# A two-layer hybrid block with routed experts: token rows scattered by slot into DRAM instead of gathered by a one-hot product

## The reference

```python
def moe_swiglu(h, w_router, wg, wu, wd):
    logits = (h @ w_router).astype(jnp.float32)
    top_v, top_i = lax.top_k(logits, TOP_K)          # TOP_K = 2 of 8
    top_p = jax.nn.softmax(top_v, axis=-1)
    gates = jnp.sum(jax.nn.one_hot(top_i, N_EXPERTS, dtype=jnp.float32) * top_p[..., None], axis=-2)
    act = jax.nn.silu(jnp.einsum('bnd,edf->bnef', h, wg)) * jnp.einsum('bnd,edf->bnef', h, wu)
    act = act * gates.astype(h.dtype)[..., None]
    return jnp.einsum('bnef,efd->bnd', act, wd)
# h = x * (1 + scale) + shift;  x <- LayerNorm(alpha * x + gate * moe_swiglu(h))
```

## Time and profile before

| what | value |
|---|---|
| runs | 1744.07, 1744.25, 1749.58 us |
| profiled execution | 1745.37 us, span of its instructions 1743.5 us |
| TensorE busy | 1551.2 us, 89% |
| VectorE, ScalarE busy | 761.9 us (44%), 575.6 us (33%) |
| DMA | 425.14 MB, mean 244 GB/s |
| granted TensorE clock, mean | 0.946 |
| expert loop | from 878 to 1708 us |
| chain that ended last | TensorE 75%, DMA 7%, VectorE 6%, SyncE's DMA issues 6% |

### The profile page before, as it was taken

One profiled execution on the slowest core, in us unless ns is written; L12 is line 12 of the kernel. 1 busy time (PEld: TensorE's weight loads), 2 busy tenths in 40 slices (PEclk: granted clock), 3 DMA queues, 4 the chain that ended last, 5 costly groups with the idle time before them and its releaser, 6 DMA issues.

```text
span 1743.5 us, 24616 instructions
## 1 busy us (share of the span) xinstructions
PE 1551.2 (89%) x9147; PEld 1033.1 (59%) x9148; DVE 761.9 (44%) x1228; ACT 575.6 (33%) x979; POOL 75.9 (4%) x92
## 2 busy tenths in 40 slices
PE   4798989999999898989886699989999899999771
PEld 1584567888887585566622366645555577677220
DVE  0483776433333664675700255524544443244115
ACT  0432554332221442451200344433433433233101
POOL 2010001000000010020000000000000000000002
PEclk8799999999999899999789799999999999999896
DMA  9235535442442444565499999999999578677993
GB/s 334 98 133 179 194 121 189 147 139 83 140 145 91 176 145 161 193 194 177 172 379 387 333 389 395 387 382 386 380 337 366 215 286 290 210 270 261 387 389 114
DMA packets 216738, 425.14 MB, mean 244 GB/s; under 512 B 15656, under 2 KB 65832, under 8 KB 216592
## 3 DMA queue, kind: packets, MB, share of 16 engines
q1 hardware_dynamic: 197792, 395.35, 62.7%
q0 software_dynamic: 5264, 18.04, 3.2%
q10 hardware_dynamic: 13536, 9.83, 1.8%
HBM read 406.93 MB, written 16.25 MB: 243 GB/s over the span
## 4 chain that ended last, share of the span: by engine, by line
PE 75%; DMA 7%; DVE 6%; SPq 6%; issue 3%; ACT 3%; ACTq 1%; POOL 0%; DVEq 0%; POOLq 0%
PE ps L2004 27%; PE ps L2406 6%; PE ps L2323 5%; PE ps L2324 4%; PE ps L2327 4%; SPq L717 4%; PE ps L2400 3%; PE ps L2452 3%; DMA hT<-h_columns 2%; PE ps L1936 2%; PE ps L2348 2%; DMA ring<-in_w_moe_up 2%; PE ps L2351 2%; PE ps L2354 2%; PE ps L2098 2%
## 5 line engine op out<-in xcount | busy, mean ns | idle before, releaser
L2004 PE MATMUL ps<-d_ring_parts,scratch_parts 128*128 128x512 f32 (+1 forms) x444 | 172.2, 388 | 13.9 <-DVE hT_parts L1296 9.1
L2400 PE MATMUL ps<-ring,hT 128*64 128x512 f32 (+1 forms) x576 | 128.3, 590 | 38.0 <-issue 21.0
L1840 DVE TENSOR_TENSOR cst<-cst,ps 128x256 f32<-128x256 f32 (+2 forms) x89 | 32.8, 369 | 254.5 <-ACT cst L1151 254.5
L2004 PE MATMUL ps<-gu_ring_parts,scratch_parts 128*128 128x512 f32 (+1 forms) x336 | 128.7, 383 | 0.0
L2406 PE MATMUL ps<-ring,hT 128*32 128x256 f32 x1760 | 117.2, 385 | 7.5 <-DMA hT<-h_columns 7.5
L2004 PE MATMUL ps<-d_ring_parts,hT_parts 128*128 128x512 f32 (+1 forms) x312 | 119.2, 382 | 0.0
L2400 PEld LDWEIGHTS ps<-ring,hT 128*64 128x64 f32 x576 | 40.8, 144 | 112.3 <-issue 84.7
L2004 PEld LDWEIGHTS ps<-d_ring_parts,scratch_parts 128*128 128x128 f32 x444 | 84.8, 191 | 32.2 <-issue 9.3
L2004 PE MATMUL ps<-gu_ring_parts,o_parts 128*128 128x512 f32 x264 | 103.2, 391 | 0.0
L1176 ACT ACTIVATE qkv_parts<-ring 128x1024 fp32r<-128x1024 f32 x102 | 103.1, 1050 | 0.0
L2406 PEld LDWEIGHTS ps<-ring,hT 128*32 128x32 f32 x1760 | 56.3, 110 | 56.5 <-issue 23.8
(11 more groups left out here) (383 smaller groups left out, 3119.8 us busy)
## 6 DMA issues: line engine op xcount, KB each, us to landing
ring<-in_w_moe_gate SPq DMA_DIRECT2D x176, 512.0 KB, 9.9
ring<-in_w_moe_up SPq DMA_DIRECT2D x176, 512.0 KB, 11.4
ring<-in_w_moe_down SPq DMA_DIRECT2D x176, 512.0 KB, 9.8
gu_ring<-in_w_ada SPq DMA_DIRECT2D x48, 1024.0 KB, 7.5
gu_ring<-in_w_in SPq DMA_DIRECT2D x16, 1024.0 KB, 7.3
gu_ring<-in_w_ffn_gate SPq DMA_DIRECT2D x11, 1024.0 KB, 5.4
gu_ring<-in_w_ffn_up SPq DMA_DIRECT2D x11, 1024.0 KB, 7.9
d_ring<-in_w_ffn_down SPq DMA_DIRECT2D x11, 1024.0 KB, 9.8
```

What stands on the lines that cost most here:

```text
L2004: ins = pe.matmul(out, a, w, start=(start and n == 0), stop=(stop and n == 2))
L2400: ins = pe.matmul(ps[64 * j:64 * j + 64, bank, 0:2 * f].rearrange("p (a f) -> p a f", a=2), hT[:, kc, col:col + 64], wt[:, :, f * j:f * j ...
```

## The change

The one-hot table, its product with the rows, the splitting of the rows and the store of the columns go. In their place:

- GpSimd clears a second table in DRAM, `h_table` (1152 rows of 4 KB), with nine DMAs ahead of the ten clears of `y_rows`. After the mixer's norm it stores x in `x_kept`, and when the slots are known, it scatters each tile's rows of h to the two slots of each token: six indirect DMAs.
- x's buffer in SBUF now holds, during the loop, the rows of h of the next body. ScalarE loads them from `h_table` with four DMAs: for the first body after the scatters, and for each other body in step 2 of the body before it.
- TensorE turns rows into columns by transposes into PSUM, from where ScalarE and VectorE copy halves to `hT`: the base (8 transposes) before the last down product of the body before, the other 256 rows (16 transposes) at the common top, before the first gate-up product, and only where the body has a full group. The top now waits for the result's copies first, since those transposes write PSUM banks 0 to 3.
- In the last body x comes back from `x_kept`, and `fold` waits for it.
- SyncE loads granules 10 to 15 right after granule 0.

```diff
             sp.wait_ge(ada_expanded, 32)
             load_granule((0, 0), 0)
-            for first, last, n in ((0, HALF_SLOTS, 4), (HALF_SLOTS, SLOTS_PADDED, 8)):
...
-                sp.dma_start(h_columns[:, :, first:last], hT_all[:, :, first:last]).then_inc(columns_stored, 16)
-            sp.wait_ge(gather_mm, 16)
-            load_granule((0, 0), AHEAD - 1)
-            sp.wait_ge(columns_stored, 32)
...
-            for pos in range(10, AHEAD - 1):
+            sp.wait_ge(stored, 128)
+            for pos in range(10, AHEAD):
                 load_granule((0, 0), pos)
...
                 if l == 1:
+                    for r0 in range(0, SLOTS_PADDED, P):
+                        pool.dma_start(h_table[r0:r0 + P, :].rearrange("r (c f) -> r c f", f=P),
+                                       cst[:, C_ONES:C_ONES + P].unsqueeze(1).broadcast_to([P, KD, P])
+                                       ).then_inc(table_cleared, 16)
                     for r0 in range(0, ROWS_MAX, P):
...
+            pool.dma_start(x_kept, x[:, :, :].rearrange("p i d -> p (i d)")).then_inc(x_stored, 16)
+            pool.wait_ge(table_cleared, 16 * (SLOTS_PADDED // P))
+            pool.wait_ge(slots_ready, 1)
+            for i, n in ((2, 4), (0, 6), (1, 6)):
+                pool.wait_ge(hTok_copied, n)
+                for a in range(2):
+                    pool.indirect_dma_start(h_table[:, :], bass.IndirectOffsetOnAxis(ap=slot_at[:, i, a:a + 1], axis=0),
+                                            h_rows[:, i, :], None).then_inc(rows_scattered, 16)
+            pool.wait_ge(rest_turned, NE)
+            pool.wait_ge(x_stored, 16)
+            pool.dma_start(x[:, :, :].rearrange("p i d -> p (i d)"), x_kept).then_inc(x_back, 16)
...
+            def load_rows(at):
+                for where_at, tall, p0, i in zip(at, (P, P, 64, 64), (0, 0, 0, 64), (0, 1, 2, 2)):
+                    act.dma_start(x[p0:p0 + tall, i, :], h_table[where_at, :]).then_inc(rows_landed, 16)
+
+            def base_columns(n):
+                act.wait_ge(base_turned, n)
+                act.activation(hT[:, 0:4, 0:P], ps[:, 6, :].rearrange("p (k t) -> p k t", k=4), ACT.Copy).then_inc(base_act, 1)
+
+            act.wait_ge(rows_scattered, 16 * 2 * NT)
+            act.wait_ge(x_stored, 16)
+            act.wait_ge(xT_mm, 16)
+            load_rows([slice(0, P), slice(P, 2 * P), slice(2 * P, WIDEST), slice(WIDEST, TOKENS)])
+            base_columns(1)
...
+                        if k == 2 and partner:
+                            act.wait_ge(rest_turned, t + 1)
+                            act.wait_ge(rest_turned, t + 1).then_inc(rows_landed, 16 * LOADS)
+                            next_rows(t + turns)
...
+            def turn_rows(i, banks):
                 for kc in range(KD):
...
+                    ins = pe.transpose(ps[:, banks[kc // 4], P * (kc % 4):P * (kc % 4) + P], x[:, i, P * kc:P * kc + P], ident)
+                return ins
...
+                        if k == len(steps):
+                            pe.wait_ge(hidT_copied, s0 + turns * STEPS)
...
+                                turn_next(t + turns)
...
                 with pe.If(variant > 1):
-                    pe.wait_ge(hT_base, t * 16 + 16)
+                    pe.wait_ge(y_act, t * HELD + HELD)
+                    pe.wait_ge(y_dve, t * HELD + HELD)
+                    turn_rows(1, (0, 1))
+                    turn_rows(2, (2, 3)).then_inc(rest_turned, 1)
+                    pe.wait_ge(base_act, t + 1)
+                    pe.wait_ge(base_dve, t + 1)
```

More of the change, by code:

```diff
@@ L82 @@
 D_GRANULES = 10
-GATHER_BANKS = [0, 1, 2, 3]
+LOADS = 4
 ROW_BANKS = [4, 5, 6, 7]
@@ L1110, in _ @@
                     act.activation(expo[:, :, :], expo[:, :, :], ACT.Exp).then_inc(expo_ready, 1)
-            COLUMNS = [(T_BASE, 0, P, hT_base), (T_REST, P, WIDEST - P, hT_rest), (T_PART, WIDEST, TOKENS - WIDEST, hT_part)]
-            def fetch_columns(t, which):
-                for at, c0, w, landed in which:
-                    first = act.value_load(sched[0:1, bass.ds(t + at, 1)], min_val=0, max_val=SLOTS_PADDED - w)
-                    act.dma_start(hT[:, :, c0:c0 + w], h_columns[:, :, bass.ds(first, w)]).then_inc(landed, 16)
@@ L1849, in expert @@
                     turned_rest(len(steps) - 1)
+                if partner:
+                    dve.wait_ge(base_turned, t + 2).then_inc(base_dve, 1)
+                    base_columns(t + turns + 1)
+                else:
+                    with dve.If(t < NE - 1):
+                        base_columns(t + turns + 1)
+                if partner:
+                    dve.wait_ge(rest_turned, t + 2).then_inc(rest_dve, 1)
+                if ng == 0:
+                    dve.wait_ge(rest_turned, t + 1).then_inc(rest_dve, 1)
                 y0 = t * HELD + HELD * (turns - 1)
@@ L1869, in first_product @@
                 with dve.If(variant > 1):
+                    dve.wait_ge(rest_turned, t + 1)
+                    for q in range(2):
+                        ins = dve.tensor_copy(hT[:, 4:8, P + P * q:2 * P + P * q],
+                                              ps[:, 2 * q + 1, :].rearrange("p (k t) -> p k t", k=4))
+                    ins.then_inc(rest_dve, 1)
                     dve.wait_ge(sil_ready, t * STEPS + (DENSE + 1))
```

207 lines of the change are left out of this document (79 added, 128 removed).

## The result

The changed kernel takes 1750.15 us (median of 11 runs, 1746.41 to 1756.62), the kernel before beside it 1742.23 us (median of 11). The ratio is 1.0036, 95% interval 1.0020 to 1.0052: slower, as forecast, but by half of what I had: 6 us instead of 12.

The account below looks back on a forecast made before the run. TensorE and DMA were taken as both full in pair bodies B and C, with TensorE standing between bodies. The terms summed to +12.0 us on 1744.3, forecasting 1756 us, range 1737 to 1775.

Parts of the forecast that it names:

- term 4: Start of the first pair body (B): rows already in SBUF, so the fetch waits go; -15.6 us.
- term 5: Starts of the second and third pair bodies (C, D): transposes wait for result copies; +3.1 and +1.1 us.
- term 8: First pair body (B): weight ring enters about five granules shorter after a shorter pause; +1 us, bounds 0 and 8.
- term 1: Before the mixer's last norm: nine more clears delay the norm's bias on GpSimd's queue; +18.9 us, bounds 0 and 24.
- Norm to A: Last norm to first body (A): scatters, row loads, transposes and loop entry take 51.4 us, before 57.4.
- term 3: First body (A): 6.1 us of ring waits go, transposes add 1.9 and a branch 1; -3.2 us.
- term 6: Ends of the three pair bodies (B, C, D): transposes of the next base, 1.9 us each; +5.7 us.
- term 7: Third step of pair bodies (B, C, D): ScalarE's table reads and DMA issues partly delay weight splitting; +3 us, bounds 0 and 12.
- term 9: Last body (E): x's return from DRAM, less a dropped column fetch, +3 us; branches around unneeded transposes, +1.
- the norm isn't pushed: Mixer's last norm: parameters land with the old delay, -18.9 us, 1737; chance 0.12. By half: 11.5 us, 1749; chance 0.10.
- the 15 us of third-step issues: Pair bodies (B, C, D): ScalarE's DMA issues held up, 6 us each into the split's chain; +15, 1771; chance 0.12.
- The routing is quicker: Norm to first body: half the loop's entry overlaps and scatters land at once; up to -9 us, 1747; chance 0.08.

Follow-up runs that it names:

- e2: Kernel before, with nine clears of an unused DRAM table put ahead of its ten; ratio to the kernel before 1.0146.
- e1: Changed kernel with its 19 clears spread over the three steps of the attention before; ratio to the kernel before 0.9993.
- e8: Kernel before, with its ten clears of the result's table spread over the three steps of the attention; ratio to the kernel before 1.0002.
- e3: Changed kernel with the ten clears of y_rows moved behind the six scatters; ratio to the kernel before 1.0017.
- e4: Changed kernel with 64 more transposes, results unread, at the end of the first body; ratio to the kernel before 1.0065.
- e5: Changed kernel with the next body's rows fetched ten steps before a pair body's last step, not at its third; ratio to the kernel before 1.0039.
- e9: Changed kernel with clears spread, next rows fetched ten steps before a pair's end, last 6 of 16 granules held until rows land; ratio to before 0.9922.
- e10: Changed kernel with 160 more transposes, results unread, at the end of the first body; ratio to the kernel before 1.0114.
- e7: Changed kernel with clears spread, next rows fetched ten steps before a pair's end, last 4 of 16 granules held until rows land; ratio to before 0.9972.
- e11: Changed kernel with clears spread and the last 6 of 16 granules held until rows land, rows fetched at third step; ratio to the kernel before 0.9949.

## Why the prediction was wrong

The direction and the largest term were right. **The step that failed is the cost of the bodies' starts, terms 4 and 5.** I had -15.6 + 4.2 = -11.4 us, and the marks show -24.1 - 0.4 = -24.5. I took TensorE's work there from rows in which the granted clock was low: 0.50 for the transposes of the earlier trace rows, and 0.73, 0.72 and 0.81 for the base products of B, C and D (9.6, 9.8 and 8.8 us). In the changed kernel's profile the transposes stand ahead of the base product, and this runs at 1.00 and takes 7.0 us each time, 7.1 us less over the three. At B the copies and branches ahead of them took 1.5 us and not 5.5. What B's start won beyond the forecast the stream of weights took back (term 8, of which I saw 1 us in 7.5); what C and D won stayed. The sizes, with what the marks and runs show:

1. **The clears, +18.9: right.** +20.0 in the changed kernel, +20.2 in e2. By the Trainium skill, page "DMA: Bandwidth & Descriptors", section "Anatomy of one DMA — SWDGE (gpsimd) path", an estimate by bytes over 436 GB/s gave +10; e2's norm, 20.2 us later, disagrees with it.
2. **Norm to A, 51.4 us: 48.4 measured.** Between roots and A's first matmul the stretch shrank by 9.1 us. Scatters landed in 6.4 us and loads in 7.3, near the sum; the loop's entry took 4.9 us instead of 9.8. What I had not seen is that this price hangs on term 1: it is low because the clears had let the ring fill first. e1 shows the other price, 10.6 us more. A part of the 9.1 us may be the profiled execution's own, since e2 and e8 have 3 us more than the kernel before here.
3. **A, -3.2: -2.3, near by luck.** The 6.1 us of ring waits did not vanish, 4.9 stayed. Against that, the transposes and the wait ahead of them cost 1.3 us and not 2.9, and the rest of A's products took 2.4 us less, at a mean granted clock of 0.97 instead of 0.94. I let the weights flow at 380 GB/s from A's start. But the ring was full then, and loads can only follow what A frees: 211 GB/s in its first 20 us (389 before, in 882 to 902 us).
4. **Start of B, -15.6: -24.1.** From A's last matmul to the first turn 12.1 us instead of 36.3. I had 9.6 us for the base product, as in the earlier trace rows, where TensorE had stood 17 us and the product's mean granted clock was 0.73; now TensorE stands 1.5 us, the clock stays at 1.00 (2.4 GHz) and the product takes 7.0. The 16 transposes took 1.8 us, not 3.7, at 1.00 too. Copies and branches took 1.5 us, not 5.5; of these, no row shows the 2.5 us that I had added for ScalarE's code. The product's clock is 1.00 at B in e1, e3, e4, e5, e9 and e10 as well.
5. **Starts of C and D, +3.1 and +1.1: +0.4 and -0.8.** The transposes and the wait for copies are there (3.5 and 4.0 us at C), as in the sum, at a granted clock of 0.51 (1.2 GHz, after 4.0 us of standing), but the clock is back at 1.00 for the base product, 7.0 instead of 9.8 us and 8.8, and the fetches' waits go. This part is not steady: in e1, e3, e5 and e10 the first 7 us of C's base product have a clock of 0.81 to 0.93.
6. **Transposes of the next base, +5.7: right in sum,** not in its parts: 1.1 us of transposes (I had 1.9) and 0.8 us of waiting for ScalarE, three times.
7. **Third-step issues, +3: 7.5, and not by that cause.** The added waits for the split are 2.5 us in B and 5.0 in D. e5 takes the issues away: B keeps its length and D keeps 3.2 of its 5.0, all of it the first of the two waits. In every version with turned rows the first wait in D is 3.0 to 3.6 us. VectorE's timeline in D, after, shows it idle for 6.1 us with nothing to wait for before the split's first work (1.6 us in the kernel before):

```profile
1356.81 0.42 DVE L1856 TENSOR_TENSOR cst<-cst,ps 128x256 f32<-128x256 f32 x1 [7.30 <-ACT cst L1258]
1363.38 2.29 DVE L1791 TENSOR_TENSOR hT_parts<-hT,o_parts 128x2048 fp32r<-128x2048 f32 x1 [6.14 <-issue]
```

Why VectorE comes so late is open.

8. **The ring at B, +1: 7.5.** For the head start that I forecast, +1 holds: e4 starts B 7.5 us later, which leaves 16.6 of the 24.1 us, and its B is 164.7 us long, 0.6 more than in e10 (164.0), where 5.7 us are left. The changed kernel's is 171.5 us long for 158.6 before: 7.5 are the head start lost to the ring (against e10), 1.9 are term 6, 2.5 are term 7, 1.0 has no name. I had written that in B and C both TensorE and the DMA are full, and then priced a shorter ring by the length of the pause alone, with no end to what a shorter pause can win. The end is in a pause of the stream that my two windows, which meet at 985 us, don't show. In the kernel before SyncE issued nothing for 12.3 us at B's start, 9.8 of them waiting for TensorE to free a granule: B's late start had let the ring fill. From 985 to 993 us the DMA moved 219 GB/s.

```profile
980.70 0.41 SPq L717 DMA_DIRECT2D ring<-in_w_moe_up  x1
993.00 2.22 SPq L723 DMA_DIRECT2D ring<-in_w_moe_down  x4
```

So the 88th to the 100th of the 528 loads took 30.3 us. In the changed kernel they take 19.4, with no such pause; e4 has none either, and in e10 it is back, 12.5 us. From the 40th load to the 352nd, issued 3.4 us before C's last matmul, the changed kernel's weights flow at 368 GB/s (360 before). The stream won the 11 us of the pause, and from A's last matmul to B's last TensorE won as much, 11.3 us. By the 352nd load the stream is 4.9 us ahead of before, and not 15.

9. **E, +4: -0.6.** E's entry after D took 14.5 us instead of 11.2, but the rest was 3.9 us shorter: TensorE waited 5.4 us for weights there instead of 9.6, so the bytes that I had charged don't show. The same code entered E in 9.0 us in e4 and 13.6 in e5, so this part of the ledger is only known to some 5 us; what sets it is open. E's first matmul after:

```profile
1638.07 12.24 PE L2380 MATMUL ps<-ring,hT 128*64 128x512 f32 x48 [14.49 <-issue]
```

The parts: 10.9 - 2.3 - 24.1 - 0.4 + 5.7 + 7.5 + 7.5 + 2.1 (1.0 in B, 0.4 in C, 0.7 in D, unnamed) - 0.6 = +6.3. Against the forecast: terms 1 and 2 together -2.0, term 3 +0.9, term 4 -8.5, term 5 -4.6, term 7 +4.5, term 8 +6.5, term 9 -4.6, unnamed +2.1, in all -5.7. Terms 4 and 8 nearly cancel (-2.0 left), and not by chance: what B's start wins beyond the ring's room, the ring takes back. Of what is left, term 5's -4.6 and term 7's +4.5 cancel by chance, and term 9's -4.6 is no larger than what E varies by. Of term 5 the low granted clock of the rows is shown; of term 7 the cause is open.

Of the rivals, "the norm isn't pushed" fell by e2, and so did its half, 11.5 us; "B's start isn't gained" fell by the marks, and the 15 us of third-step issues by e5, which takes them away and changes the time by nothing. "The routing is quicker" was right in its half of the loop's entry, 4.9 us for 9.8; but in e3, e7, e9 and e11 the entry took 7.5 to 7.8 us, so it isn't shown to be an overlap. Of the signs, "no wait for ring weights in A" was wrong, and 12 us from A's last matmul to B's first turn were not the 20.

## What to carry to other kernels

Where the DMA is full on both sides of a stall, removing the stall gives back only as much as the stream stood during it, here 11 of the 24 us by which B's first turn moved: look for that standing time first, in windows that don't cut through it, and price the gain by it. Look at the granted clock beside each row that a price is taken from: the same product took 9.8 us at 0.72 and 7.0 at 1.00. A wait that looks long can be covered by another that ends just after it; it then costs nothing to keep, nothing is won by removing it, and all that is added to it shows. And small transfers on a critical path should be let through before a prefetch that has slack: the queue that fills the ring had to be held 6 granules short, not 4, since what is already issued still stands ahead.

## What the hardware showed unexpectedly

- Clears of 512 KB in pieces of 512 bytes hold up the engine that issues them: GpSimd issues seven in 6.2 us and then stands 10.3 us, later 12.8. No run has other pieces.
- From the last of the same six scatters to the row loads that wait for them it took 6.4 us where the fill's last load had been issued 5.9 us ahead of the first scatter, 8.7 with six granules held back, and 12.0 to 12.8 inside the fill or with four held back. The four row loads took 7.3 to 7.4 us, 11.9 beside the fill, and 14.3 us beside fill and clears.
- The way into the first body took TensorE 4.9 to 7.8 us in kernels whose loop is the same, and into the last body 9.0 to 14.9 us, with no wait that the profile names. What sets it is open.
- 16 matmuls of 128x512 took 7.0 us at a granted clock of 1.00, and 9.6, 9.8 and 8.8 us at a mean of 0.73, 0.72 and 0.81, after TensorE had stood 17.2, 2.7 and 3.2 us. 16 transposes took 1.9 us at 1.00 after 1.5 us of standing, and 3.5 and 3.6 us at 0.51 and 0.50 after 4.0 and 3.4 us.
